# Routing rounds, gathered rows and their order dealt anew beside the foreground of a hybrid encoder step

## The reference

```
proj = x @ w_in                                  # q, k, v, latents, gates
o_a  = stick_breaking_attend(...); o_b = mla_attend(...)      # 8 heads each
h    = layer_norm(ALPHA * x + (sig(g_a) * (o_a @ w_oa) + sig(g_b) * (o_b @ w_ob)) @ w_out)
# PEER: 8 heads, 16 of 16384 experts each
s    = einsum(h @ wq, sub_keys)                  # 2 x 128 scores a token and head
experts, top_s = top 16 of the sums of the two top-16 lists
g    = softmax(top_s)
ff   = sum over heads and k of  g * gelu(u[expert] . h) * v[expert]
y    = layer_norm(ALPHA * h + ff)
```

## Time and profile before

| | us |
|---|---|
| median of 3 runs | 3416.0 |
| the profiled execution | 3423.4 |
| its span, first to last instruction | 3421.6 |
| three groups' foreground stages | 0 to 2005 |
| project, stick, mla_project, mla of group 1 | 476, 673, 800, 854 to 962 |
| merge, scores of group 1 | 962, 1069 to 1188 |
| project, stick, mla_project, mla of group 2 | 1188, 1373, 1562, 1606 to 1771 |
| merge, scores of group 2 | 1771, 1878 to 2005 |
| dense stage | 2005 to 3422 |

### The profile page before, as it was taken

One profiled execution on the slowest core, in us unless ns is written; L12 is line 12 of the kernel. 1 busy time (PEld: TensorE's weight loads), 2 busy tenths in 40 slices (PEclk: granted clock), 3 DMA queues, 4 the chain that ended last, 5 costly groups with the idle time before them and its releaser, 6 DMA issues. The chain is left out here.

```text
span 3421.6 us, 35761 instructions
## 1 busy us (share of the span) xinstructions
PE 2957.4 (86%) x10191; PEld 1655.9 (48%) x10191; DVE 2399.6 (70%) x4846; ACT 1215.1 (36%) x3120; POOL 1554.7 (45%) x1180
## 2 busy tenths in 40 slices
PE   8989869766788799677678969999989999999993
PEld 5755645433445455443444635544445555455541
DVE  0121387696957878787768578787878787888877
ACT  0241243375642333775654232222222222322221
POOL 0000147664744488876878663333333333333330
PEclk9988989888689899888889989999999999999996
DMA  4575869867889999658679999999999999999994
GB/s 149 198 250 194 283 224 355 320 224 242 276 292 380 349 350 378 197 155 223 183 221 312 334 351 416 415 415 415 415 416 415 415 415 415 415 415 413 414 408 168
DMA packets 374853, 1096.91 MB, mean 321 GB/s; under 512 B 91616, under 2 KB 209344, under 8 KB 288512
## 3 DMA queue, kind: packets, MB, share of 16 engines
q0 software_dynamic: 164784, 750.26, 58.7%
q1 hardware_dynamic: 176800, 303.85, 25.0%
q10 hardware_dynamic: 33072, 40.51, 3.4%
HBM read 1031.18 MB, written 62.23 MB: 320 GB/s over the span
## 5 line engine op out<-in xcount | busy, mean ns | idle before, releaser
L455 POOL DMA_INDIRECT expert_rows<-in_experts,picked_index x524 | 623.0, 1189 | 907.9 <-DVE ff_sum L609 798.7
L597 DVE SCALAR_TENSOR_TENSOR expert_rows<-expert_rows,h_tile 128x1024 f32<-128x1024 f32 x556 | 678.7, 1221 | 255.9 <-DMA expert_rows<-in_experts,picked_index 245.1
L478 POOL DMA_INDIRECT gates_by_expert<-dense_gate,gate_address x384 | 687.8, 1791 | 159.8 <-issue 113.9
L609 DVE SCALAR_TENSOR_TENSOR ff_sum<-expert_rows,coefficients,ff_sum 128x1024 f32<-128x1024 f32 x556 | 712.5, 1281 | 43.4 <-ACT coefficients L560 42.2
L1824 PE MATMUL dense_out_ps<-dense_value_rows,dense_weights 128*128 128x512 f32 x1536 | 692.1, 601 | 51.4 <-DVE dense_weights L1902 51.4
L1835 PE MATMUL dense_act_ps<-dense_hT,key_columns 128*128 128x384 f32 x2048 | 684.5, 488 | 24.0 <-PEq L1636 21.4
L1835 PEld LDWEIGHTS dense_act_ps<-dense_hT,key_columns 128*128 128x128 f32 x2048 | 388.9, 191 | 328.0 <-issue 69.9
L1824 PEld LDWEIGHTS dense_out_ps<-dense_value_rows,dense_weights 128*128 128x128 f32 x1536 | 295.4, 193 | 402.6 <-issue 311.7
L554 ACT ACTIVATE activated<-dots 128x1 f32<-128x1 f32 (+1 forms) x624 | 125.1, 200 | 927.2 <-DVE expert_rows L597 682.1
L866 PE MATMUL proj_ps<-xT,w_in_block 128*128 128x384 f32 (+1 forms) x1392 | 420.1, 465 | 39.5 <-PEq L1636 26.7
L866 PEld LDWEIGHTS proj_ps<-xT,w_in_block 128*128 128x128 f32 x1392 | 267.7, 193 | 191.4 <-issue 45.8
(11 more groups left out here) (195 smaller groups left out, 3179.2 us busy)
## 6 DMA issues: line engine op xcount, KB each, us to landing
key_columns<-in_key_columns SPq DMA_DIRECT2D x128, 512.0 KB, 32.5
dense_value_rows<-in_experts SPq DMA_DIRECT2D x128, 512.0 KB, 29.3
gates_by_expert<-zeros POOLq DMA_DIRECT2D x12, 2048.0 KB, 21.9
wq_half<-in_peer_wq SPq DMA_DIRECT2D x48, 512.0 KB, 10.8
dense_gates<-gates_by_expert SPq DMA_DIRECT2D x128, 192.0 KB, 31.1
w_in_block<-in_w_in ACTq DMA_DIRECT2D x18, 1024.0 KB, 9.7
w_in_block<-in_w_in SPq DMA_DIRECT2D x18, 1024.0 KB, 8.3
w_out<-in_w_out SPq DMA_DIRECT2D x24, 512.0 KB, 7.2
```

Of the source, the lines that this page charges most:

```text
L455: pool.indirect_dma_start(to, None, self.a["experts"], bass.IndirectOffsetOnAxis(ap=index[:, k:k + 1], axis=0)).then_inc(got, 16)
L478: pool.indirect_dma_start(self.a["gates_by_expert"], bass.IndirectOffsetOnAxis(ap=self.flat[i][:, k:k + 1], axis=0), self.dgate[i][:, k:k ...
L597: dve.scalar_tensor_tensor(place, place, 1.0, self.h[n % 2][:], ALU.mult, ALU.mult, accum_out=self.dots[:, s % TOPK:s % TOPK + 1]).then_in ...
L609: dve.scalar_tensor_tensor(total, self.slots[self.slot_of[p]][:, D:2 * D], self.coef[:, y % TOPK:y % TOPK + 1], total, ALU.mult, ALU.add). ...
```

## The change

Two edits, both to tables; no instruction of the foreground changes. `SHARES` deals rows and rounds anew. Rows beside project fall from 44 and 39 (groups 1 and 2) to 30 and 25, those beside stick rise from 24 and 28 to 29 and 37, beside mla_project from 8 and 7 to 11 and 9, beside mla from 22 and 25 to 28 and 31. Rounds beside project rise from 7 and 8 to 10 and 13; stick loses all (2 and 5), mla_project its 1 and 1, mla falls from 2 and 5 to 0 and 2; merge and scores take 2 + 2 more in group 1 and 1 + 1 in group 2. The dense stage keeps 21 rounds and gets 395 row steps for 391. `routes` deals the rounds of tiles 4, 2 and 3 as two of tile 4 in five, where it was one in three. The last number of each share, the scatters, moves too.

```diff
-        ((1, "project"), 44, 1, 7, 44), ((1, "stick"), 24, 2, 2, 24), ((1, "mla_project"), 8, 1, 1, 10), ((1, "mla"), 22, 2, 2, 24),
-        ((1, "merge"), 22, 1, 0, 20), ((1, "scores"), 27, 1, 3, 16),
-        ((2, "project"), 39, 1, 8, 56), ((2, "stick"), 28, 2, 5, 60), ((2, "mla_project"), 7, 1, 1, 20), ((2, "mla"), 25, 2, 5, 56),
-        ((2, "merge"), 16, 1, 2, 34), ((2, "scores"), 28, 1, 3, 30),
+        ((1, "project"), 30, 1, 10, 56), ((1, "stick"), 29, 2, 0, 30), ((1, "mla_project"), 11, 1, 0, 10), ((1, "mla"), 28, 2, 0, 32),
+        ((1, "merge"), 20, 1, 2, 12), ((1, "scores"), 24, 1, 5, 20),
+        ((2, "project"), 25, 1, 13, 80), ((2, "stick"), 37, 2, 0, 60), ((2, "mla_project"), 9, 1, 0, 14), ((2, "mla"), 31, 2, 2, 56),
+        ((2, "merge"), 16, 1, 3, 36), ((2, "scores"), 26, 1, 4, 34),
...
-        self.routes = [*ahead(0, 1), (SAMPLE, 0), (SAMPLE, 4), *heads(4, 2, 3), *heads(5), *heads(6), *heads(7)]
+        own, others = heads(4), heads(2, 3)
+        turns = [(own if 2 * (i + 1) // 5 > 2 * i // 5 else others).pop(0) for i in range(20)] + others
+        self.routes = [*ahead(0, 1), (SAMPLE, 0), (SAMPLE, 4), *turns, *heads(5), *heads(6), *heads(7)]
```

## The result

| | before | after |
|---|---|---|
| median of 4 runs each, same chip | 3416.56 us (3414.84 to 3421.89) | 3454.32 us (3452.0 to 3456.77) |
| span of the profiled execution | 3421.6 us | 3450.3 us |

The account below looks back on a forecast made before the run. POOL's issue of indirect DMAs was taken to bound mla of group 2 and tie PE in project of group 2, DMA and PE level in dense. Terms -6 + 0 + 26 - 2 + 0 - 16 + 0 + 4 + 10 = +16: 3432 us, range 3400 to 3456.

Parts of the forecast that it names:

- Project of group 1, -6: Project, group 1: POOL's work +6, its 14.5 us behind DVE gone, a wait inside +2; -6 us, bounds -18 and 0.
- The five other stages of group 1, 0: Stick through scores, group 1: DVE's idle time hides its added work and POOL has rest; 0 us, bounds -8 and +12.
- Project of group 2, +26: Project, group 2: POOL's issue of 80 scatters for 55 lengthens the stage; +26 us, bounds -3 and +33.
- Mla of group 2, -16: Mla, group 2: POOL stops bounding, DVE's waits go (-24), ACT's table loads add 8; -16 us, bounds -30 and -4.
- Stick of group 2, -2: Stick, group 2: 9 more gathers, 5 fewer loads, rounds gone, ACT table loads added; -2 us, bounds -12 and +10.
- Merge, 0: Merge, group 2: one more round and 9 fewer scatters change nothing; 0 us.
- Scores, +4: Scores, group 2: 8 more scatters, 2 fewer gathers, 13 us on POOL partly hidden by rest; +4 us, 0 to +13.
- Mla_project of group 2, 0: Mla_project, group 2: POOL's program work falls from 54 to 43 us, about the stage's 44; 0 us.
- Dense, +10: Dense stage: 4 more row steps paid at 415 GB/s, late scatters cost 0; +10 us, bounds 0 and +14.
- the hidden issue: Rival, project of group 2: queue hands excess on to mla, project ends with PE, -4 for +26; 3402 us, chance 0.20.
- dense that pays nothing: Rival, dense stage: the 4 rows fit between PE's work, 10 us fall away; +6, 3422 us, chance 0.10.
- The starving backlog: Rival, group 2: backlog starves rows and rounds, project +33, stick +8, mla only -10; +39, 3455 us, chance 0.12.

Follow-up runs that it names:

- the light edit: Kernel before, group 1 alone given the changed kernel's rows and rounds in project, stick, mla_project and mla, scatters near before: 3397.12 us for 3419.8, ratio 0.9929.
- the last experiment: Kernel before with 9 rows, no round, 14 scatters in mla_project of group 2, 37 rows and 9 rounds in project, 2 scatters late in dense: ratio 0.9998.
- the 56-scatter kernel: Changed kernel without late scatters in dense, 24 scatters moved from project of group 2 (56 for 80) to mla of group 2: ratio 1.0189 to the kernel before.
- the kernel with 24 rows in scores: Kernel before with 24 rows for 28 in scores of group 2, 395 row steps for 391 in dense, no late scatters: ratio 0.9993.
- the scatters spread: Changed kernel without late scatters in dense, group 1's scatters moved from stick, mla_project and mla into merge and scores: ratio 1.0074 to the kernel before.
- the kernel with old scatters: Changed kernel's rows, rounds and order, each stage's scatters set near the numbers of before, none in dense: ratio 1.0097 to the kernel before.

## Why the prediction was partly right

Right were the sign and the bound of project of group 2, the stage that I took for the largest. The time fell into the range of 3400 to 3456, but only since I had drawn that up to a rival's 3455; the forecast's own 3422 to 3444 was missed: +38 us came for +16. The step that failed is the zeros. I had put the five other stages of group 1 (measured +21.0), mla_project of group 2 (+8.1) and the late scatters in dense at nothing, because POOL had rest, DVE idle time and PE loaded keys to hide them. The relief of mla of group 2 failed too, -16 for which -3.6 came. That project of group 2 came out 17 us below its term covered part of this, and that was luck.

- **Project of group 1, -6.** Measured -12.3, inside its bounds. PE's closing wait fell from 18.2 to 6.7 us, as the bound said. The terms were others than mine: the 14.5 us behind DVE, which were to fall away, are still 13.4. What fell is POOL's busy time, from 138.65 to 130.88, where I had POOL's work rise by 6: 53 scatters fell into the window, not 56, at 1.70 us for 1.82, and 16 fewer gathers, not 14.
- **The five other stages of group 1, 0.** This step failed; they made +21. *Mla*, +10.6: at 14 to 24 scatters it takes 109 to 115 us (six kernels with 28 rows and no round), at 27 it takes 119 to 120 (four kernels, which have the same program up to there). I had written that POOL has rest there, but by my own prices its program came to 27 x 2.05 + 28 x 1.59 = 100 of 109 us. POOL also can't use all its rest: it works in order, and what a blocked instruction holds back can be a gather. *Scores*, +7.8: every kernel with 5 rounds there has 126 to 128 us, every one with 3 has 117 to 120, with POOL at 56.57 of 126.5. That is 4 us a round, near the 5.2 that DVE works for one, so DVE's idle time seems not to have hidden it; those kernels also have 3 rows fewer and 13 to 15 scatters for 5 to 10, and no kernel moved the rounds alone. *Stick*, -0.4: in the light edit, with both rounds gone, five rows more and one scatter more, it took 114.9, 12 us less; six scatters more gave back 8.6 of them. The term was -12 + 12, not 0 and 0.
- **Project of group 2, +26.** The mechanism held (POOL's waits are nearly all issue, PE idles 15.8 us, and it is 182.3 us once the scatters go). The size was +9.0, for three reasons. Alone in the same window the 75 scatters that fell into it take 127.71 us and 25 gathers 27.96, so 1.70 and 1.12 each where I had 1.75 and 1.29 (without the 0.3): some 8 us. The score loads add 8 us to that, not 13. And the 80 scatters of the program left 75 in the window: five more went past its end than came in, 10 us by my price.
- **Mla of group 2, -16.** This failed. DVE's waits for rows fell to 6.9, but the stage went down by only 3.6, no more than equal programs differ by. With 31 scatters less and the rows of before it is still 160.0, and 160.3 with all 56 in the last experiment. POOL's full count (166.4 of 165) was at best a tie with the chain of the other engines and I read it as the bound; PE's wait for ACT's `probsT`, 53.1 us before, is 50.4 after. The 15.27 us that POOL stands for one round's index come on top, and 20.8 on a full ring.
- **Stick of group 2, -2:** -1.9. **Merge, 0:** -0.8. **Scores, +4:** -5.1; eight scatters more weighed less than two rows fewer. With 39 scatters it was 133 to 135 in three kernels with the same rows.
- **Mla_project of group 2, 0.** It became +8.1. Its own deal is cleared by the last experiment. PE waited 7.6 us for weights that ACT prepares late, 4.2 before (and PEld 8.4 us for the load of such weights, 4.8 before):

```profile
PE mla_ps L1196 <- ACT w_uq_rope L1222: 4.2, 1, 4.2
PE mla_ps L1198 <- ACT w_uq_rope L1224: 7.6, 1, 7.6
```

Which part of what project and stick hand on makes them late was not tried by itself, and stays open.

- **Dense, +10.** The four row steps are worth +9.7 where they alone were changed; the nine kernels with 391 row steps and no late scatter have 1410.3 to 1417.6 us, the five with 395 have 1423.6 to 1431.9. The late scatters I had at 0, because PE has five blocks of keys loaded, "some 50 us". That size was wrong: PE was through them in 27.57 us, and then stood 19.1. Taking the scatters away gave 7.3 us back, but in the last experiment a wait of 13.1 us left dense as it was, so how much of the rest of the +16.5 they made stays open.

The sum as it was measured: -12.3 + 21.0 + 9.0 - 1.9 + 8.1 - 3.6 - 0.8 - 5.1 + 16.5 = +30.9, with -2.3 in the first group +28.6, the difference of the spans to 0.1. The medians differ by 9 us more than the two profiled executions, so this sum leaves 9 of the 38 us unplaced.

Of the rivals, the hidden issue is refuted by the 56-scatter kernel (-15 us in project), and dense that pays nothing by the kernel with 24 rows in scores (+9.7). The starving backlog gave nearly the measured time, but not by its mechanism: project was +9, not +33. By the Trainium skill (DMA: Bandwidth & Descriptors, "Issuing engines are not separate DMA queues") issuing takes a sequencer's time that is usually small beside the DMA. In project of group 2 the trace shows it the other way as far as it matters for the time: POOL is full from end to end, with 22.5 + 7.5 us of fixed steps and 164.04 busy in 194.5, and the scatters move 128 numbers each. The traces give no time for such a transfer itself.

Whether the changed kernel's loss is the issue itself or POOL's order has an answer only in part. Shown: in project of group 2 it is issue. In merge of group 1 with the scatters spread and in mla_project of the kernel with old scatters POOL has time left (68.61 of 131; PE done 23 us early) and the stage is still longer, with gathers and scatters blocked behind one another in POOL's order. That this order is the cause there is read from timelines; no kernel separated the two kinds of work, so it is argued and not shown.

## What to carry to other kernels

Work that shares an in-order queue is not priced by its sum against the queue's rest. Ask which instruction each blocked one holds up: here a full ring held the scatters, and a scatter that waited for an index or for landed ones held the gathers. A queue that is full in a stage may only be level with the chain beside it; take the work off it in one experiment before forecasting what relief is worth. When several stages are dealt anew at once, try one group at a time: here one half, with the scatters of each stage moved by at most five, was worth -0.7%, and the whole cost +1.0%.

## What the runs showed that I had not expected

- The price of a scatter depends on its place: 10.3 us for the five moved into scores of group 2 of the changed kernel, 8.6 for six into stick of group 1 of the light edit (2.1 and 1.4 us each), nothing for two at the start of dense, and 31 us for 14 in scores of group 2 of the kernel before, where POOL became full.
- Four rows are worth 9.7 to 12.6 us in dense and 11.8 to 12.1 in scores of group 2: 2.4 to 3.2 us a row, near the 2.5 us that its 1.05 MB takes at the 415 GB/s of dense.
- Identical programs of a stage differ between kernels that differ only elsewhere: mla of group 1 took 110.8 and 114.8, mla_project of group 1 54.1 and 62.9. Yet the times of one kernel's executions agree within 0.5%, so what is handed from stage to stage seems to settle differently with each program; no run tested that.
